# A streaming encoder step with a mixture of experts: the last stage's elementwise work divided between VectorE and Pool

## What is computed

```python
x = x + g1 * mix
h = rms_norm(x, p["norm2_g"]) * (1 + sc2) + sh2
x = x + g2 * grouped_moe(h, p["w_router"], p["b_router"], p["w_exp_gate"], p["w_exp_up"], p["w_exp_down"])
return x, rows
```

## Time and profile before

| | |
|---|---|
| median of 3 runs | 1188.93 us (1186.75 to 1189.68) |
| the profiled execution's own time | 1187.63 us |
| its span in the trace | 1185.8 us |
| PE busy | 1068.2 us (90%) |
| DVE busy | 389.4 us (33%) |
| POOL busy | 143.5 us (12%) |

### The profile page before, as it was taken

How to read it: one execution, slowest core, us unless ns; L and a number is a source line. 1 busy time by engine, 2 the same in 40 slices (tenths; PEclk the granted TensorE clock), 3 DMA queues, 4 the chain that set the end, 5 groups by cost and what they waited for, 6 DMA issues and landing times.

```text
span 1185.8 us, 21577 instructions
## 1 busy us (share of the span) xinstructions
PE 1068.2 (90%) x8635; PEld 714.0 (60%) x8635; DVE 389.4 (33%) x894; ACT 244.0 (21%) x486; POOL 143.5 (12%) x218
## 2 busy tenths in 40 slices
PE   5899999989979979889999999955999999999991
PEld 4445764456745757667677754425676767677770
DVE  2100738956777655200000003353111111111114
ACT  4111232127745335200000001121111101010100
POOL 0000210110000000200000010010222222222221
PEclk9999999999979989999999999976999999999996
DMA  9542855345000248880030027066796996999935
GB/s 344 221 149 88 311 170 189 110 122 193 1 1 1 72 144 283 231 232 1 19 123 1 1 99 293 36 220 223 256 305 204 358 366 215 316 381 373 382 93 195
DMA packets 103029, 217.05 MB, mean 183 GB/s; under 512 B 9477, under 2 KB 17749, under 8 KB 102694
## 3 DMA queue, kind: packets, MB, share of 16 engines
q1 hardware_dynamic: 91446, 184.42, 43.5%
q0 software_dynamic: 11504, 31.52, 9.8%
HBM read 196.87 MB, written 19.05 MB: 182 GB/s over the span
## 4 chain that ended last, share of the span: by engine, by line
PE 79%; DVE 8%; DMA 5%; ACT 4%; issue 3%; SPq 0%; DVEq 0%; POOL 0%; ACTq 0%; POOLq 0%
PE ps L2105 17%; PE ps L1996 10%; PE ps L1651 10%; PE ps L2116 9%; PE ps L2007 6%; PE ps L2051 4%; PE ps L1677 3%; PE ps L1696 3%; PE ps L1595 3%; PE ps L1625 2%; DMA mem<-in_w_branch_b 2%; DMA mem<-in_x_sample 2%; PE ps L1778 2%; PE ps L2110 1%; ACT mem L952 1%
## 5 line engine op out<-in xcount | busy, mean ns | idle before, releaser
L2105 PEld LDWEIGHTS ps<-mem 128*64 128x64 f32 x3584 | 198.5, 138 | 24.8 <-issue 21.4
L2105 PE MATMUL ps<-mem 128*64 128x128 f32 x3584 | 209.5, 275 | 2.1 <-DVE mem L1552 0.9
L1996 PE MATMUL ps<-mem 128*128 128x320 f32 x512 | 139.2, 433 | 1.1 <-DVEq L1359 1.1
L1996 PEld LDWEIGHTS ps<-mem 128*128 128x128 f32 x512 | 97.3, 190 | 41.5 <-issue 1.3
L1651 PE MATMUL ps<-mem 128*128 128x512 f32 (+1 forms) x320 | 113.3, 514 | 1.8 <-ACT mem L912 0.9
L2116 PE MATMUL ps<-mem 128*64 128x512 f32 x448 | 107.1, 597 | 4.2 <-DVE mem L1566 0.5
L1651 PEld LDWEIGHTS ps<-mem 128*128 128x128 f32 x320 | 54.2, 191 | 58.5 <-issue 58.5
L1595 PE MATMUL ps<-mem 128*128 128x128 f32 x432 | 66.9, 294 | 22.8 <-DVE mem L1129 8.8
L1397 DVE TENSOR_TENSOR mem<-mem,ps 128x320 f32<-128x320 f32 x32 | 15.6, 488 | 198.1 <-PE ps L2007 198.1
L1564 DVE TENSOR_TENSOR mem<-mem,ps 128x128 f32<-128x128 f32 x56 | 16.1, 288 | 186.9 <-PE ps L2105 186.9
L1595 PEld LDWEIGHTS ps<-mem 128*128 128x128 f32 x432 | 53.4, 151 | 36.7 <-DVE mem L1129 9.8
(11 more groups left out here) (288 smaller groups left out, 1141.3 us busy)
## 6 DMA issues: line engine op xcount, KB each, us to landing
mem<-in_w_exp_gate SPq DMA_DIRECT2D x16, 2048.0 KB, 12.5
mem<-in_w_exp_up SPq DMA_DIRECT2D x16, 2048.0 KB, 17.9
mem<-in_w_exp_down SPq DMA_DIRECT2D x16, 2048.0 KB, 22.3
mem<-in_w_ada SPq DMA_DIRECT2D x12, 2048.0 KB, 14.4
mem<-in_w_in SPq DMA_DIRECT2D x9, 2048.0 KB, 13.1
mem<-in_cache_b_k SPq DMA_DIRECT2D x8, 1024.0 KB, 5.6
mem<-in_cache_b_v SPq DMA_DIRECT2D x8, 1024.0 KB, 8.5
mem<-in_w_out SPq DMA_DIRECT2D x2, 2048.0 KB, 11.4
```

The costliest lines, as they stand in the source:

```text
L1996: last = mm(b[:, 0:320], w[:, k, P * (m % 4):P * (m % 4) + P], hT[:, k, 320 * h:320 * h + 320], start=(k == 0), stop=(k == KD - 1))
L2105: last = mm(b[UNIT * h:UNIT * h + UNIT, 0:P], x_, w[:, k, 256 * h + P * c:256 * h + P * c + P], start=(k == 0), stop=(k == KD - 1), skip_g ...
```

## The change

The columns of each tile are divided at CUT = 704: VectorE does the gate product and the residual sum on columns 0 to 703, Pool on columns 704 to 1023. Pool does so after it has raised `y_all`, tile by tile, and counts its sums on a new semaphore, `e_out_pool`. SP waits for both before it stores a tile. Both engines wait for the arrival of `g2` first, VectorE did not have that wait before.

```diff
         zeros = view(O_TMP + 8470, 1024)
+        CUT = 704
...
         later_ready = sem("later_ready")
+        e_out_pool = sem("e_out_pool")
...
             for t in range(NT):
                 sp.wait_ge(e_out, 100 + t + 1)
+                sp.wait_ge(e_out_pool, t + 1)
                 sp.dma_start(out_rows("y", t), ysum[t]).then_inc(out_st, 16)
             sp.wait_ge(out_st, 16 * NT)
...
             pool.sem_inc(y_all, 1)
+            pool.wait_ge(g2_ld, 16 * (1 + DEC_B))
+            for t in range(NT):
+                pool.wait_ge(tile_ld[t], 32)
+                c = ysum[t][:, CUT:D]
+                own(g.tensor_tensor(c, c, g2[t == SMP][:, CUT:D], ALU.mult))
+                own.settle()
+                g.tensor_tensor(c, c, x1[:, t, CUT:D], ALU.add).then_inc(e_out_pool, 1)
             pool.wait_ge(rows_st, 160)
...
+            dve.wait_ge(g2_ld, 16 * (1 + DEC_B))
             for t in range(NT):
                 dve.wait_ge(tile_ld[t], 32)
-                c = ysum[t]
-                step(v.tensor_tensor(c, c, g2[t == SMP], ALU.mult))
-                v.tensor_tensor(c, c, x1[:, t, :], ALU.add).then_inc(e_out, 1)
+                c = ysum[t][:, 0:CUT]
+                step(v.tensor_tensor(c, c, g2[t == SMP][:, 0:CUT], ALU.mult))
+                v.tensor_tensor(c, c, x1[:, t, 0:CUT], ALU.add).then_inc(e_out, 1)
```

## The result

The kernel after takes 1198.05 us in the median of 8 runs, the kernel before 1187.73 us in 8 runs beside it: ratio 1.0079, 95% interval 1.0058 to 1.0099. By this ratio it is some 9.4 us slower; the two medians lie 10.3 us apart. The prediction was 1192.9 us, 4.0 us slower, with a range up to 1195.0. The direction was forecast; the size is more than twice the forecast and outside the range.

The account below looks back on a forecast made before the run. The last stage was taken as bound by VectorE, with DMA not far behind. Alternating at 3.22 us a tile, 16.1 us against 12.08, added 4.0 us to the median 1188.93, giving 1192.9 us; range 1185.5 to 1195.0.

Parts of the forecast that it names:

- the added waits: Last stage: g2 waits, SP's wait for Pool before stores, Pool's tile waits and the shared load semaphore all cost nothing.
- the prediction's own signs of being wrong: Terms set to nothing are wrong if, among others, SP waits long for Pool when Pool's sum has ended.
- The likeliest case: Last stage: VectorE and Pool alternate, 3.22 us a tile, 16.1 us for five, +4.0 us; chance 0.45.
- The lower end, columns only: Cheapest price of alternating: only columns count, all of the fixed part hidden; 2.80 us a tile, 13.99 us, +1.9 us.
- The Trainium skill's rule: Two-SBUF-input VectorE and SBUF-reading GpSimd instructions need the same ports; the first keeps them its whole length, the other stands still.
- Side by side: Rival, last stage: Pool has its own way to SBUF, both keep their lengths; -3.1 us, 1185.8 us; chance 0.27.
- VectorE first, Pool after: Rival, last stage: Pool finds no gap until VectorE finishes its five tiles; +5.65 us, 1194.6 us; chance 0.15.
- Finely shared reading: Rival, last stage: both engines stretch but run together; at most +1.9 us, 1189 to 1190.8 us; chance 0.13.
- the bound of 0.3%: Difference of 3.6 us, about what a measurement tells from none; slower begins at 1192.5, faster ends at 1185.4.
- the loads and stores: Last stage's tile transfers: they take nothing from the 3.1 us gain without disturbance, but leave no more to win.
- the g2 wait: Both engines wait for g2 rows, issued by 793 us, over 300 us ahead: costs nothing.

Follow-up runs that it names:

- alone (+6.6): Kernel before with one wait added: Pool, computing nothing in the last stage, waits for VectorE's last sum before its closing part; 1196.1 us, ratio 1.0052.
- shortened (4.6 us of 9.25 gone): Kernel after with two explicit Pool drains added earlier, at 267 us and behind the g2 row issues at 793 us; 1193.42 us, ratio to before 1.0034.
- hidden (+0.5 left): Kernel after with Pool's share cut down to tile 0, tiles 1 to 4 VectorE's alone; 1190.38 us, ratio 1.0004.

## Why the prediction was wrong

**The step that failed** is the one on the added waits: "Pool's wait for a tile holds up only its closing waits on row stores ... All nothing". Behind those waits stands Pool's closing drain, 9.3 us, and behind that the end of the program. It was in the trace of before, at line 142, in the very stage that I read, and hidden under VectorE's work: it ended at 1176.7, 8.9 us before SP was done. I took "Pool is idle" from the windows, which do not count a drain as busy. Its exposure is 6.5 of the 9.25 us. With the 6.6 us that the wait alone cost, the sum comes out: 15.14 + 2.7 + 6.6 = 24.4 against 24.39. The runs show it three ways: alone (+6.6), shortened (4.6 us of 9.25 gone), and hidden (+0.5 left). One of the prediction's own signs of being wrong came true with it: SP waits 6.6 us for Pool after Pool's last sum has ended.

**The likeliest case was right, its size was not.** The engines alternate; the forecast priced it at 3.22 us a tile, +4.0 us, and it measured 2.93 us and +2.7. The lower end, columns only, gave 2.80; what is added to it is 0.02 us a turn for VectorE and 0.05 for Pool. I had charged 0.077 us of fixed part to VectorE from two instructions in a row on one engine and 0.13 to Pool from an addition with a DMA issue behind it; by the 0.02 and 0.05 us measured, most of this part runs beside the other engine's instruction. This error, 1.3 us too much, hid a little of the drain's 6.5. The Trainium skill's rule (SBUF — State Buffer, SBUF: two separate sides) is borne out here, with its limit to Pool instructions that read SBUF: the memset was free, the copy was not. That the loser waits for the whole of the other's instruction is a little more than these rows show: in turns 704 columns cost 0.75 us, and not the 0.89 that the instruction takes alone.

**The rivals.** Side by side is refuted at this form of operands, and happens with the second tensor in PSUM. VectorE first, Pool after did not occur: a Pool instruction that waits gets the next turn each time. Finely shared reading would have given the same total as alternating without fixed parts, and 0.1 us a tile separates them; that each end follows the other by one instruction's columns decides for turns. Had there been no drain, the time would have been some 2.7 us over before, no difference by the bound of 0.3%. The drain stands behind Pool's last sum in every one of these cases, so it was missing from all their prices: even side by side, with Pool's end at 1179.6 by the prediction's own sum, a drain of 9.3 us would have ended at 1188.9, behind the end of before (1185.8) and not 3.1 us ahead of it. This is an estimate; no run had five tiles side by side.

**What was right:** the loads and stores did not bind (the DMA engines were at 0.22 to 0.65 of their time from 1178 on), the g2 wait cost next to nothing (VectorE starts 0.10 us after tile 0's landing, 0.02 before), and what moved before 1167 us, 1.7 us, I take for scatter.

## What to carry to other kernels

Before an idle engine is given work at the end of a program, look at what it still has to do after its last instruction, drains included, and not only at its busy share: a late finish can cost more than the work. In these runs Pool was no relief for VectorE's two-tensor work in SBUF, at 2.08 ns against 1.04 ns a column and one at a time. It was a relief with VectorE's second tensor in PSUM (1.73 us a tile against 2.40), where PE had time to put it, and Pool's writing of constants disturbed nothing. A drain of Pool in an early idle stretch took its part off the closing one (4.8 us instead of 9.3).

## What the runs showed of the hardware that was not expected

- Pool's drain lasts 0.05 us right behind another drain and 3.34, 4.80 and 9.31 us behind 40, 58 and 134 DMAs issued by Pool, although the transfers have landed by then.
- A wait of SP at the program's end was put down to PE's queue (6.6 us), with PE's own closing step over 25 us earlier; Pool was the late one.
- VectorE's instruction with one tensor and a constant, for which the expectation had left both outcomes open, and Pool's reading exclude each other as well (1.22 us against 0.53).
